# Twelve adaptive units of a second block: four stay in an attention loop, eight move in halves into a chunk stage and a recurrence

## What is computed

```python
mod = silu(c) @ w_mod + b_mod          # 1024 x 6144: sh1, sc1, gt1, sh2, sc2, gt2
mod_c = silu(c_ctx) @ w_mod + b_mod    # for the context rows
c_in = rms_norm(ctx, norm1_g) * (1 + csc1) + csh1     # context: streams and states only
a_in = rms_norm(x, norm1_g) * (1 + sc1) + sh1
# gated delta rule in chunks of 64, two directions, context first, its states feed x
h = x + gt1 * mix_out(...)             # w_out
f_in = rms_norm(h, norm2_g) * (1 + sc2) + sh2
out = rms_norm(h + gt2 * expert_choice_ffn(f_in), final_norm_g)   # 16 experts
```

## Time and profile before

| | |
|---|---|
| median of 3 runs | 1199.15 us (1196.9 to 1199.96) |
| the profiled execution's own time | 1196.62 us |
| its span | 1194.8 us |
| TensorE busy | 1019.4 us (85%) |
| VectorE, ScalarE busy | 435.5 us (36%), 240.4 us (20%) |
| the DMA queue of the stream | 314.18 MB, 64.1% of 16 engines' span |
| chain that ended last | PE 58%, DMA 33%, DVE 5%, issue 2% |

### The profile page before, as it was taken

How to read it: one execution, slowest core, us unless ns; L and a number is a source line. 1 busy time by engine, 2 the same in 40 slices (tenths; PEclk the granted TensorE clock), 3 DMA queues, 4 the chain that set the end, 5 groups by cost and what they waited for, 6 DMA issues and landing times.

```text
span 1194.8 us, 18373 instructions
## 1 busy us (share of the span) xinstructions
PE 1019.4 (85%) x7810; PEld 530.9 (44%) x7810; DVE 435.5 (36%) x1031; ACT 240.4 (20%) x590; POOL 55.2 (5%) x70
## 2 busy tenths in 40 slices
PE   5999999999899989999998789997666767667666
PEld 2344764444476447885677765432111211112111
DVE  0137656423865527355258682411000000000002
ACT  0012144111214513535122252100000000000002
POOL 0101000000100000001213300000000000000000
PEclk9999999999999999999999999999889888898789
DMA  9963248443326984014322016999999999999996
GB/s 381 419 274 141 98 184 331 165 158 141 141 104 265 430 328 159 1 71 152 132 73 73 4 71 265 411 419 431 430 429 431 429 429 429 430 429 428 432 429 286
DMA packets 28161, 323.69 MB, mean 271 GB/s; under 512 B 3265, under 2 KB 3393, under 8 KB 5809
## 3 DMA queue, kind: packets, MB, share of 16 engines
q1 hardware_dynamic: 26048, 314.18, 64.1%
q0 software_dynamic: 2032, 8.35, 2.0%
HBM read 321.47 MB, written 1.05 MB: 270 GB/s over the span
## 4 chain that ended last, share of the span: by engine, by line
PE 58%; DMA 33%; DVE 5%; issue 2%; ACT 1%; SPq 1%; DVEq 0%; ACTq 0%
PE banks L650 48%; DMA ring<-in_stream 18%; DMA zuv_to_Kt<-in_stream 9%; DMA scr_qk<-in_stream 3%; DMA Vt_to_O<-in_stream 3%; PE banks L661 3%; PE banks L917 1%; SPq L553 1%; PE banks L938 1%; PE banks L2223 1%; PE banks L903 1%; PE banks L900 1%; PE banks L800 1%; DVE KC L1253 0%; PE banks L908 0%
## 5 line engine op out<-in xcount | busy, mean ns | idle before, releaser
L650 PE MATMUL banks<-ring,uT 128*128 128x512 f32 (+1 forms) x512 | 223.5, 590 | 7.2 <-DVE uT L1120 2.9
L650 PEld LDWEIGHTS banks<-ring,uT 128*128 128x128 f32 x512 | 95.5, 191 | 119.6 <-issue 112.7
L650 PE MATMUL banks<-scr_qk 64*64 64x64 f32 (+4 forms) x2368 | 92.8, 268 | 23.2 <-DMA scr_qk<-in_stream 17.3
L650 PE MATMUL banks<-ring,scr_qk 128*32 128x512 f32 (+1 forms) x496 | 84.4, 635 | 27.2 <-DMA ring<-in_stream 26.6
L2794 DVE SCALAR_TENSOR_TENSOR UWK<-UWK,banks 128x256 f32<-128x256 f32 x16 | 6.7, 421 | 261.9 <-ACT UWK L3080 261.9
L650 PE MATMUL banks<-ring,UWK 128*32 128x512 f32 (+1 forms) x336 | 85.2, 762 | 13.5 <-ACT UWK L3088 8.1
L650 PEld LDWEIGHTS banks<-scr_qk 64*64 64x64 f32 (+3 forms) x2368 | 64.7, 136 | 52.2 <-issue 39.4
L3080 ACT ACTIVATE UWK<-banks 128x256 f32<-128x256 f32 x16 | 6.1, 384 | 360.8 <-PE banks L650 360.8
L650 PE MATMUL banks<-UWK,ring 128*128 128x256 f32 x320 | 71.0, 380 | 0.0
L2223 PE MATMUL banks<-UWK 128*128 128x512 f32 x128 | 64.9, 630 | 0.9 <-DVE UWK L2802 0.9
L650 PEld LDWEIGHTS banks<-UWK,ring 128*128 128x128 f32 x320 | 60.4, 190 | 9.3 <-issue 1.4
(11 more groups left out here) (384 smaller groups left out, 1220.5 us busy)
## 6 DMA issues: line engine op xcount, KB each, us to landing
ring<-in_stream SPq DMA_DIRECT2D x93, 2048.0 KB, 14.5
scr_qk<-in_stream SPq DMA_DIRECT2D x11, 2048.0 KB, 39.4
Vt_to_O<-in_stream SPq DMA_DIRECT2D x11, 2048.0 KB, 39.7
zuv_to_Kt<-in_stream SPq DMA_DIRECT2D x10, 2048.0 KB, 39.4
scr_qk<-in_stream SPq DMA_DIRECT2D x11, 1024.0 KB, 40.9
wide<-in_stream SPq DMA_DIRECT2D x10, 1024.0 KB, 38.5
const<-in_stream SPq DMA_DIRECT2D x10, 1024.0 KB, 37.6
misc<-in_stream SPq DMA_DIRECT2D x10, 1024.0 KB, 39.4
```

The lines of the kernel that those rows point to most:

```text
L650: return pe.matmul(o, a, b, start=start, stop=stop)
```

## The change

Only the first four units (sh1, sc1) stay in the attention loop. The other eight come after the z, u, v units in the stream and are multiplied in halves of 4 matmuls into bank 4: halves 0 to 10 between the levels of chunk stage 1, halves 11 to 15 between Q S and the wait for `Vnew` in the recurrence. Bank 4 is held by them for that time, so that U, K V, W S and the mixer use other banks. The rows of the late units are copied by ScalarE, turned into columns, spread and used in `pe_mix2`, where the work on gt1, the router and `pe_const_logits` now stands. On SyncE the third unit of the first expert is issued before the fifth late unit.

```diff
+EARLY_MODS = 4
@@ unit_order
-            for cg in range(12):
+            for cg in range(EARLY_MODS):
                 cols("w_mod_2", 0, cg * 512, 512, "mod_mm", cg)
...
         cols("w_in_2", 0, Z_COL + i * 512, 512, "zuv_mm", i, 1)
+    for cg in range(EARLY_MODS, 12):
+        cols("w_mod_2", 0, cg * 512, 512, "mod_mm", cg)
     for cg in range(2):
         cols("w_out_2", 0, cg * 512, 512, "y2_mm", cg, 1)
@@ SyncE
-            for k in range(len(units)):
+            first, late = units.index(("gu_mm", 0, 0)), units.index(("mod_mm", EARLY_MODS + 4))
+            for k in [*range(late), first + 2, *range(late, first + 2), *range(first + 3, len(units))]:
@@ new
+        def pe_mod_late(pe, *halves):
+            for i in halves:
+                n, half = i // 2, i % 2
+                if half == 0:
+                    late_w[n] = take(pe)
+                if i == 0:
+                    pe.wait_ge(*free(4))
+                    pe.wait_ge(*at("late_window"))
+                for j in range(4):
+                    k = 2 * j + half
+                    ins = pe.matmul(bank[4][32 * j:32 * j + 32, :], latewin[:, k, 7 - n:39 - n], late_w[n][:, k, :],
+                                    start=i == 0, stop=i == 15)
...
@@ pe_attend
-                        for n in range(12 * (m - 2) // 9, 12 * (m - 1) // 9):
+                        for n in range(EARLY_MODS * (m - 2) // 9, EARLY_MODS * (m - 1) // 9):
                             pe_mod_rows(pe, n)
@@ v_mod_window
+            dve.memset(latewin[:, :, :], 0.0).then_inc(*tick("vector_step"))
...
+            dve.tensor_copy(latewin[:, :, 7:8], modwin[:, :, MOD_AT:MOD_AT + 1]).then_inc(*tick("vector_step", "late_window"))
@@ pe_streams
-                if j == 7:
-                    pe_grow(pe, 0)
@@ pe_chunks
+        def u_banks(s, t):
+            return (0, 1) if t == 0 else (5, 0) if s else (4, 5)
...
                 if s and 1 <= n <= 3:
                     pe_ctx_WS(pe, n)
+                if s and n:
+                    pe_mod_late(pe, 2 * n - 1)
...
                 if s and n <= 3:
                     pe_ctx_KV(pe, n)
+                if s:
+                    pe_mod_late(pe, 2 * n)
@@ pe_ctx_KV
-            pe_both_KV(pe, 0, n, (4, 0), new_v if n else first_v)
+            pe_both_KV(pe, 0, n, (5, 0), new_v if n else first_v)
@@ pe_recur
+                pe.wait_ge(*free(0))
...
-                        ins = pe_WS(pe, r, r, n, h)
-                        if h == H2 - 1:
-                            ins.then_inc(*fill(r, "WS_mm", 1, n, r))
+                        ins = pe_WS(pe, 0, r, n, h)
+                ins.then_inc(*fill(0, "WS_mm", 1, n))
...
+                pe_mod_late(pe, *((11,), (12, 13), (14,), (15,))[n])
                 for r in range(2):
                     pe.wait_ge(*at("Vnew", 1, n, r))
...
-            pe_const_logits(pe)
@@ pe_mix2
             pe_m2T(pe, 1, 1)
+            pe_late_columns(pe)
+            pe_grow(pe, 0, 0)
             pe_y2(pe, w, 0, 0, 1)
+            pe_grow(pe, 0, 1)
             pe_y2(pe, w, 0, 1, 1)
             pe_y2(pe, w, 1, 0, 1)
+            pe_const_logits(pe)
@@ v_mix2 (VectorE, ahead of the first product with grow)
+            v_mod_late(dve)
+            v_grow(dve, 0)
+            v_router(dve)
@@ v_streams
-            v_router(dve)
...
-                if j == 8:
-                    v_grow(dve, 0)
@@ a_mix2
+            act.wait_ge(*at("mod_mm", 11))
+            act.activation(modrows[:, :], bank[4][:, :], ACT.Copy).then_inc(*drain(4, "late_rows"))
```

More of the change, by code:

```diff
@@ L677, in pe_mod_rows @@
         def pe_mod_rows(pe, n):
-            pe_rows(pe, ("mod_mm",), modwin, MOD_AT, 2, n, 0, 11, 7)
+            pe_rows(pe, ("mod_mm",), modwin, MOD_AT, 2, n, 0, EARLY_MODS - 1, 7)
+        late_w = {}
+        def pe_mod_late(pe, *halves):
[10 more added lines that the diff above has]
+                                    start=i == 0, stop=i == 15)
+                event = ("mod_mm", EARLY_MODS + n)
+                if i == 1:
+                    ins.then_inc(*fill(4, *event))
+                elif half:
+                    ins.then_inc(*tick("bank4_filled", *event))
+                    K.events[("use", *event)] = K.events["use", "mod_mm", EARLY_MODS]
         def pe_ada_columns(pe, l, half=0):
@@ L1712, in pe_mod_columns, with pe_late_columns, pe_grow @@
             for m in range(4):
-                ins = mm(pe, bank[7][:, m * 24:(m + 1) * 24], modrows[:, m * P:(m + 1) * P], C("spread")[:, 0:24], True, True)
+                ins = mm(pe, bank[7][:, m * 8:(m + 1) * 8], modrows[:, m * P:(m + 1) * P], C("spread")[:, 0:8], True, True)
             ins.then_inc(*fill(7, "mod_cols"))
[L1716 to L1719, removed]
+        def pe_late_columns(pe):
+            pe.wait_ge(*free(0))
+            pe.wait_ge(*at("late_rows"))
+            for m in range(4):
+                ins = mm(pe, bank[0][:, m * 8:(m + 1) * 8], modrows[:, m * P:(m + 1) * P], C("spread")[:, 0:8], True, True)
+            ins.then_inc(*fill(0, "late_cols"))
+        grow_banks = ((1, 0), (7, 5))
+        def pe_grow(pe, i, h):
+            b = grow_banks[i][h]
+            pe.wait_ge(*free(b))
+            mm(pe, bank[b][:, :], row_of(6 * i + h), modrows[:, :], True, True).then_inc(*fill(b, "grow_mm", i, h))
         def pe_ctx_T(pe):
@@ L1944, in pe_chunks @@
                 pe.wait_ge(*at("bV", s, t))
-                for b in range(4):
-                    pe.wait_ge(*free(4 * t + b))
+                for b in (*u_banks(s, t), 4 * t + 2, 4 * t + 3):
+                    pe.wait_ge(*free(b))
                 bV = scr[:, t, AT_:M_ + 1, :].rearrange("p a n -> p (a n)")
@@ L2025, in pe_recur @@
             for n in range(4):
+                pe.wait_ge(*free(0))
                 for r in range(2):
-                    pe.wait_ge(*free(r))
                     pe.wait_ge(*at("state", *((1, n - 1, r) if n else (0, 3, r))))
@@ L2148, in pe_route @@
             ins.then_inc(*fill(5, "affT_mm"))
-            pe_grow(pe, 1)
+            pe_grow(pe, 1, 0)
+            pe_grow(pe, 1, 1)
             pe.wait_ge(*at("O", 3, 0))
@@ L2303, in v_mod, with v_mod_late @@
                     dve.wait_ge(*drained(7))
[L2304 to L2308, removed]
+            dve.tensor_scalar(mod[:, 8:16, :], mod[:, 8:16, :], 1.0, None, ALU.add).then_inc(*tick("vector_step"))
+            dve.wait_ge(*last("vector_step"))
             dve.tensor_tensor(A1, mod[:, 8:16, :], over(PR("n1g"), 2), ALU.mult).then_inc(*tick("vector_step"))
+            dve.wait_ge(*last("vector_step"))
+        def v_mod_late(dve):
+            dve.wait_ge(*at("late_cols"))
+            dve.tensor_tensor(mod[:, 16:48, 0].rearrange("p (c m) -> p c m", m=4),
+                              bank[0][:, 0:32].rearrange("p (m c) -> p c m", m=4),
+                              PR("bmod")[:, 16:48].rearrange("p (c m) -> p c m", m=4), ALU.add).then_inc(*drain(0))
+            dve.wait_ge(*drained(0))
+            dve.tensor_scalar(mod[:, 32:40, 0], mod[:, 32:40, 0], 1.0, None, ALU.add).then_inc(*tick("vector_step"))
             dve.wait_ge(*last("vector_step"))
@@ L2323, in v_grow @@
             dve.wait_ge(*at("grow_bias", i))
-            for h, b in enumerate(((3, 5), (7, 5))[i]):
+            for h, b in enumerate(grow_banks[i]):
                 g = grow[:, h * 512:(h + 1) * 512]
@@ L2608, in v_chunks @@
                 if s and n <= 3:
-                    for r, b in enumerate((4, 0)):
+                    for r, b in enumerate((5, 0)):
                         v_state(dve, 0, n, r, b)
@@ L2636, in v_recur @@
             for n in range(4):
-                for r in range(2):
-                    dve.wait_ge(*at("WS_mm", 1, n, r))
-                    v_Vnew(dve, 1, n, r, r).then_inc(*drain(r, "Vnew", 1, n, r))
+                dve.wait_ge(*at("WS_mm", 1, n))
+                v_Vnew(dve, 1, n, 0, 0).then_inc(*tick("vector_step", "Vnew", 1, n, 0))
+                dve.wait_ge(*last("vector_step"))
+                v_Vnew(dve, 1, n, 1, 0).then_inc(*drain(0, "Vnew", 1, n, 1))
                 if n < 3:
                     v_decay(dve, 1, n)
-                    for r in range(2):
-                        v_state(dve, 1, n, r, 4 + r)
+                    for r, b in enumerate((1, 5)):
+                        v_state(dve, 1, n, r, b)
                 else:
@@ L2696, in v_mix2 @@
                     if t and cg == 0:
+                        dve.wait_ge(*at("const_mm"))
+                        dve.tensor_tensor(const_z, bank[3][:, 0:EXPERTS], RW("br"), ALU.add).then_inc(*drain(3, "const_z"))
                         v_fT(dve, 0)
```

37 lines of the change are left out of this document (19 added, 18 removed).

## The result

| | before | changed |
|---|---|---|
| median beside each other | 1199.96 us (7 runs) | 1205.16 us (7 runs) |
| ratio | | 1.0041, 95% interval 1.0022 to 1.0059 |
| profiled span | 1194.8 us | 1203.4 us |

A forecast was written before the change was run, and what follows sets the result against it. TensorE sets the pace nearly everywhere until a transfer-bound experts' tail, so the gain is how much earlier experts begin. Terms -16.7 - 1.7 + 5.9 + 0.5 + 4.3 = -7.7 us; predicted median 1191.4, 8-in-10 range 1187 to 1199.5.

The forecast's parts named there:

- At nothing: Items priced at no cost, among them SyncE's late transfers: unit 8's goes after half 1, needed over 20 us later.
- dear switching: Rival: each of 15 tiling-mode visits drains TensorE far longer; at 0.9 us more each, +5.8 us, 1205; chance 0.06.
- the gaps don't take the halves: Rival: gaps in chunk stage 1 and the recurrence stay, halves are paid in full, total 0, 1199 us; chance 0.17.
- Attention: Layer 2's attention loop, eight of twelve units removed: 53.16 us falls to 36.5, -16.7 us (bounds 13.3 to 19.1 saved).
- The pairs of layer 1: Layer 1's attention: an iteration pair with no unit, then one, takes 8.30 us; four such pairs give 33.2 us for layer 2.
- Streams: In the streams, `pe_grow(0)` is removed: -1.7 us of the 1.88 its records show.
- Ahead of chunk stage 1: Bank 5 shared by K V and Y of tile 1: Y's possible wait was bounded at 1.3 us for three levels.
- Halves 0 to 10: Chunk stage 1: eleven halves of 1.0 us, partly absorbed by TensorE's gaps, +5.9 us (bounds 4.8 to 11.0).
- The levels of 10 us: Sign in chunk stage 1: levels expected at 8.5, 8.8, 8.8, 6.3 and 9.7 us; 10 us would mean gaps stay.
- Recurrence and const_logits: Recurrence: halves 11 to 15 add 2.3 us, moving `pe_const_logits` away saves 1.8; +0.5 us (bounds +0.5 to +3.1).
- Mixing: `pe_mix2`: columns 0.8, spreading matmuls 1.7 and logits 1.8 us are added on the path, +4.3 us.
- keep its length: The experts' tail, behind SyncE's issue at 757.04: starts at about 749 with unchanged length; the prediction fails if it grows.

The follow-up runs named there:

- x2: Changed kernel without transfers of late units 8 to 11 (halves 8 to 15 reuse weights of units 4 to 7), w_out_2's transfers held until the recurrence: 1191.39 us, ratio 0.9935.
- x1: Kernel before, with only SyncE's order and four waits changed so that four of its own 2 MB transfers run in chunk stage 1: 1206.51 us, ratio 1.0066.
- x6: x5 without SyncE's wait, so the following transfers run in chunk stage 1: 1206.44 us, ratio 1.0058.
- x5: Changed kernel with only four late units (gt1, gt2), following transfers held until the recurrence's first W S: 1194.69 us, ratio 0.9965; run again 1195.44 us, 0.9968.
- x7: x5 with halves 6 and 7 moved behind Z of level 4 and between Y and Z of level 5: 1193.82 us, ratio 0.9955.
- x8: x7 with the third late unit's transfer also held until z of the first token tile is done: 1188.98 us, ratio 0.9924.

## Why the prediction was wrong

The step that failed stands under **At nothing**: "On SyncE the late units wait for halves: unit 8's transfer can go after half 1". I asked only whether a unit would come in time, and it did. I didn't ask what the transfer meets on its way, and so put its effect on TensorE at nothing; it was some 13 us of the 18.7 by which chunk stage 1 grew. (The 7.2 us that I compared with there belong to half a unit; the 2 MB into `ring` took 10.3 us in the median, and no wait came of that.) No rival named it either; the one on the slower side, dear switching, is refuted by `x2`, and so is the first one, that the gaps don't take the halves.

- *Attention*, -16.7: the loop takes 38.07 instead of 53.16, so -15.1. The pairs of layer 1 were the right pattern: three of the four take 8.30, 8.30 and 8.45 us. The first takes 10.77, with the wait of 1.81 us on ScalarE in it and a clock of 0.67 in the 5 us behind that. No wait on the ring, as said.
- *Streams*, -1.7: chunk stage 0 is 17.1 us earlier, which leaves 2.0 beside the 15.1 (0.2 of it lay ahead of the loop). Right.
- *Ahead of chunk stage 1*, not in the sum: +1.75 (622.46 - 607.60 against 637.81 - 624.70 us). I priced bank 5 for Y that waits for K V, and not for K V that waits for Y.
- *Halves 0 to 10*, +5.9 (bounds 4.8 to 11.0): +18.7. The half was right at 0.99 us, and so was the lean on the gaps: in a quiet stage the price is +4.1 (`x2`), even under the lower bound. Of the other 14.6, 1.4 lie ahead of the first transfer and 13.2 behind it. About half of the 14.6 is TensorE's idle time (9.71 against 1.89) and half its slower work (55.21 against 48.46 us busy). The levels of 10 us that I said would mean "that gaps stay" came, and the gaps did more than stay.
- *Recurrence and const_logits*, +0.5: the recurrence takes 20.54 instead of 20.10 us with five halves in it, at a clock of 1.00 instead of 0.92, and from its `ws` product to the first of `w_out_2` there are 4.4 instead of 6.2 us. Together -1.4, better than said.
- *Mixing*, +4.3: 49.82 against 45.57 us, +4.25. Right.

These make -15.1 - 0.2 - 1.8 + 1.75 + 18.7 - 1.4 + 4.25 = +6.2, and SyncE's issue of the earlier trace rows moves from 757.04 to 763.22, by just that:

```profile
763.22 1.19 SPq L556 DMA_DIRECT2D ring<-in_stream  x2
```

The tail behind it, said to keep its length, takes 440.2 us instead of 437.8, one of the signs by which the prediction was to fail. All kernels with late units have 439.4 to 440.7 there, `x1` 438.3; what it is stays open.

What is shown: transfers in the stage cost it 11 to 14 us (11.1 in `x1`, 13.2 against `x2`, 11.6 and 13.6 between `x6` and the two executions of `x5`). The gaps come by the count of instructions, they end when a packet of the instruction queue has landed, and that packet starts later while a unit is moving. Where in the queues it waits, no view shows. That the clock falls because of a gap is read from the order of rows: it is 0.64 behind 2.40 us (`x7`) and 0.72 behind 3.03 (`x1`), but still 1.00 behind 2.33 (`x6`, 672.00 to 674.70).

The row that should have warned me is in chunk stage 1 of before: gaps 125 records apart that are released by nothing, in a stage without transfers. Chunk stage 0, on which I leaned as dense "with pieces", has transfers and no gap, but that was its alignment: with 68 records fewer ahead of it (`x5`, `x6`, `x7`) it has one under a transfer at the same place, and with that transfer later (`x8`) none.

## What to carry to other kernels

When work with its own weights moves, its freed slots move too: look at what runs while the next transfer lands, and hold transfers away from stretches of short, dense matmuls (one wait in SyncE's queue was worth 11.7 us). Gaps put down to issue are worth counting in instructions: if they come at equal counts, they are a price of the stretch that grows with traffic, and that longer matmuls between them can hide. A stage's idle time is spare only as long as what causes it stays the same.

## What was not expected of the hardware

TensorE's instruction supply shows as a gap of up to 1.1 us every 126 matmul records of the 64 x 64 kind in a quiet stage, and as gaps of up to 3.65 us with 2 MB transfers in flight. In chunk stage 1 of before the block behind such a gap begins 3.8 to 4.5 us after the block ahead of it, so 126 records that need less time than that have to wait there. Eleven pieces of 1.0 us in another tiling mode take these waits in: TensorE's idle time is 1.89 instead of 7.62 us, and what is put down to issue in it 0.6 instead of 4.4. Small matmuls with long ones between them wait less than the small ones alone.
